# Two coupled transformer blocks in fp32: the turned rows of the first half moved by 32 bytes in SBUF

## The reference

```python
for l in range(2):                                  # first half; z likewise
    x = x + 0.5 * mx[2] * swiglu(modulate(rms_norm(x), mx[0], mx[1]), ffn1_w1[l], ffn1_w3[l], ffn1_w2[l])
    hx = modulate(rms_norm(x), mx[3], mx[4]) @ w_in[l]        # 1024 x 2336
    x = x + mx[5] * (token_mixing(hx, hz, ...) @ w_out[l])    # 1024 x 1024
    x = x + 0.5 * mx[8] * swiglu(modulate(rms_norm(x), mx[6], mx[7]), ffn2_w1[l], ffn2_w3[l], ffn2_w2[l])

def swiglu(h, w1, w3, w2):                          # w1, w3: 1024 x 2816; w2: 2816 x 1024
    return (jax.nn.silu(h @ w1) * (h @ w3)) @ w2
```

## Time and profile before

| | |
|---|---|
| median of 3 runs | 3195.55 us (3190.09 to 3196.07) |
| profiled execution | 3176.97 us |
| its span in the trace | 3175.2 us |
| TensorE matmul busy | 3051.7 us (96%) |
| TensorE weight load busy | 2772.3 us (87%) |
| VectorE, ScalarE, GpSimd busy | 1802.7, 1483.3 and 151.2 us |
| mean granted TensorE clock | 0.988 |
| DMA, share of 16 engines | 52% |

### The profile page before, as it was taken

One profiled execution on the slowest core, in us unless ns is written; L12 is line 12 of the kernel. 1 busy time (PEld: TensorE's weight loads), 2 busy tenths in 40 slices (PEclk: granted clock), 3 DMA queues, 4 the chain that ended last, 5 costly groups with the idle time before them and its releaser, 6 DMA issues.

```text
span 3175.2 us, 54273 instructions
## 1 busy us (share of the span) xinstructions
PE 3051.7 (96%) x23160; PEld 2772.3 (87%) x23160; DVE 1802.7 (57%) x2837; ACT 1483.3 (47%) x2222; POOL 151.2 (5%) x147
## 2 busy tenths in 40 slices
PE   7999999999999999999999999999999999999998
PEld 5899788898779997899898879999899999989997
DVE  4555554655456545545645455465766656586665
ACT  3344444453544443444444444455654445655443
POOL 0000000001000000000200000001010101111000
PEclk9999999999999999999999999999999999999999
DMA  7765444654445555765355345554355655434563
GB/s 272 283 212 171 149 151 169 216 196 145 143 153 186 174 190 192 271 222 163 133 172 166 114 159 201 189 176 134 115 161 183 198 187 164 126 111 162 173 199 133
DMA packets 409691, 556.67 MB, mean 175 GB/s; under 512 B 25276, under 2 KB 357996, under 8 KB 409068
## 3 DMA queue, kind: packets, MB, share of 16 engines
q1 hardware_dynamic: 409452, 553.20, 52.2%
HBM read 552.12 MB, written 1.05 MB: 174 GB/s over the span
## 4 chain that ended last, share of the span: by engine, by line
PE 83%; DVE 9%; ACT 3%; issue 3%; DMA 3%; SPq 0%; POOL 0%; DVEq 0%; ACTq 0%
PE psum L119 24%; PE psum L121 23%; PE psum L120 23%; DVE wl L276 1%; DMA wr<-in_ffn_w_dram 1%; PE psum L710 1%; DVE wl L2173 1%; PE psum L2338 1%; PE psum L2422 1%; PE psum L2444 1%; PE psum L1528 1%; PE psum L1183 1%; PE psum L127 1%; PE psum L1899 1%; PE psum L1515 1%
## 5 line engine op out<-in xcount | busy, mean ns | idle before, releaser
L276 DVE TENSOR_TENSOR wl<-wr,wh 128x1024 fp32r<-128x1024 f32 (+1 forms) x558 | 658.4, 1215 | 216.3 <-ACT wh L265 215.3
L265 ACT ACTIVATE wh<-wr 128x1024 fp32r<-128x1024 f32 (+1 forms) x558 | 555.0, 1039 | 249.4 <-DMA wr<-in_ffn_w_dram 219.7
L119 PE MATMUL psum<-xt_hi,wh 128*128 128x256 f32 (+1 forms) x2000 | 567.5, 284 | 4.7 <-DVE wl L276 3.7
L120 PE MATMUL psum<-xt_lo,wh 128*128 128x256 f32 (+1 forms) x2000 | 558.9, 279 | 0.0
L121 PE MATMUL psum<-xt_hi,wl 128*128 128x256 f32 (+1 forms) x2000 | 558.5, 279 | 0.0
L2173 DVE TENSOR_TENSOR wl<-wr,wh 128x1024 fp32r<-128x1024 f32 (+3 forms) x336 | 391.7, 1201 | 123.9 <-ACT wh L2165 122.6
L119 PEld LDWEIGHTS psum<-xt_hi,wh 128*128 128x128 f32 (+1 forms) x2000 | 377.7, 189 | 17.8 <-issue 10.9
L120 PEld LDWEIGHTS psum<-xt_lo,wh 128*128 128x128 f32 (+1 forms) x2000 | 377.4, 189 | 2.3
L121 PEld LDWEIGHTS psum<-xt_hi,wl 128*128 128x128 f32 (+1 forms) x2000 | 378.3, 189 | 0.1
L119 PE MATMUL psum<-wh,xt_hi 128*128 128x256 f32 (+1 forms) x1280 | 369.4, 289 | 2.8 <-ACT vv L3323 1.9
L2165 ACT ACTIVATE wh<-wr 128x1024 fp32r<-128x1024 f32 (+3 forms) x336 | 322.6, 997 | 102.4 <-DMA wr<-in_mlp_w_dram 75.2
(11 more groups left out here) (490 smaller groups left out, 5457.2 us busy)
## 6 DMA issues: line engine op xcount, KB each, us to landing
wr<-in_ffn_w_dram SPq DMA_DIRECT2D x231, 1024.0 KB, 5.2
wr<-in_w_in_dram SPq DMA_DIRECT2D x88, 1024.0 KB, 5.1
wr<-in_w_mod_dram SPq DMA_DIRECT2D x72, 1024.0 KB, 4.9
wr<-in_mlp_w_dram SPq DMA_DIRECT2D x64, 1024.0 KB, 5.3
wr<-in_w_out_dram SPq DMA_DIRECT2D x20, 1024.0 KB, 5.3
wr<-in_mem_w_kv_dram SPq DMA_DIRECT2D x8, 1024.0 KB, 5.2
wr<-in_w_branch_dram SPq DMA_DIRECT2D x16, 512.0 KB, 3.4
wr<-in_w_branch_dram SPq DMA_DIRECT2D x8, 1024.0 KB, 5.2
```

The lines of the kernel that those rows point to most:

```text
L119: pe.matmul(out, a[0], b[0], start=first, stop=False)
L120: pe.matmul(out, a[0], b[1], start=False, stop=False)
L265: act.activation(self.high[s][:, r], self.raw[s][:, r], ACT.Copy).then_inc(self.highs.sem, 1)
L276: dve.tensor_tensor(self.low[s][:, r], self.raw[s][:, r], self.high[s][:, r].bitcast(F32), ALU.subtract).then_inc(self.lows.sem, 1)
```

## The change

Three groups of tiles in the first half move by 32 bytes: the moved copies of `xt` and `zt` from 192 to 224 bytes below 80 KB and 64 KB, the scratch tiles that lie over them by as much, and the held copies from 64 to 32 bytes below 80 KB, and from 320 to 288 below 64 KB. Held less moved address becomes 128 less 32, so 96, in the up products, and 224 less 128, so 96, in the projections. The ring, the down products, `mem_t` and the second half keep their addresses. No instruction, wait or transfer is added or removed.

```diff
@@ -23,7 +23,7 @@
 SIDE_BANKS = 6
 MOD_COLS = 32
 RING_SHIFT, ROW_SHIFT = 3 / 8, 1 / 16
-MOVED_SHIFT, SIDE_SHIFT = 3 / 16, 3 / 16
+MOVED_SHIFT, HELD_SHIFT, SIDE_SHIFT = 7 / 32, 1 / 32, 7 / 32
 
 
 D_FF = 2816
@@ -3648,7 +3648,7 @@
     x = c["x"]
     pair = lambda name, kb: [at(name + "_hi", [P, KT, TOK], F32R, kb), at(name + "_lo", [P, KT, TOK], F32R, kb + 8)]
     moved = [pair("xt", 80 - MOVED_SHIFT), pair("zt", 64 - MOVED_SHIFT)]
-    held = [pair("xt", 80 - ROW_SHIFT), pair("zt", 64 - ROW_SHIFT - 1 / 4)]
+    held = [pair("xt", 80 - HELD_SHIFT), pair("zt", 64 - HELD_SHIFT - 1 / 4)]
     h = [at("hx", [P, 2, D_IN], F32, 130.5), at("hz", [P, 2, D_IN], F32, 112)]
     mix = at("mix", [P, 2, D], F32, 149)
     rows1, rows2, rtmp = at("gate_rows1", [P, D], F32, 157), at("gate_rows2", [P, D], F32, 161), at("gated_rows", [P, 512], F32, 165)
```

## The result

| | before | after |
|---|---|---|
| median of 7 runs | 3193.44 us | 3205.69 us |
| lowest and highest | 3174.26, 3196.07 us | 3197.61, 3212.65 us |
| ratio, 95% interval | | 1.0065 (1.0040 to 1.0089) |
| profiled execution | 3176.97 us | 3212.65 us |
| span in its trace | 3175.2 us | 3210.8 us |

The change makes the kernel slower by 0.65%: 21 us of 3193, with an interval of 13 to 28 us. I had forecast 14 us less. The ratio is the one on record; the two medians alone are 12 us apart (1.0038). Four runs of the kernel before were added to the three that stood ahead of the prediction; they moved its median by 2 us.

The account below looks back on a forecast made before the run. TensorE's rate of float32r products was taken to bound the kernel. All quick steps gave -14 us, other parts nothing; off the 3195.55 us median that made 3182 us, range 3168 to 3223.

Parts of the forecast that it names:

- What bounds the kernel: Whole kernel: TensorE, with matmuls in flight for 96% of the span; the rate of float32r products on lines 119 to 121.
- The two paces as states of a stretch: 256-column products: a stretch keeps the pace it gets into at its start, quick 113.3 ns or slow 117.8 ns a step.
- the step to 96 goes on in that direction: First-half up products and projections: moving away from 192 favours the quick pace, so all quick at 96, 14 us less.
- the sum: First-half up products and projections all quick at 113.3 ns, other parts costed at nothing: -14 us.
- the slower case: Lines 119 to 121, first-half up pieces: 96 behaves like 128, long stretches slow; 20 us more, 3215 us; chance 0.36.
- The chance of faster: Whole kernel: 0.44, from all quick or most of it at 0.35 and much faster at 0.09.
- wrong altogether: Sign: steps unchanged and time moving to side matmuls, writes of turned rows or low clock; or a third pace appears.
- The bound from above: First-half up products and projections: at most 118.3 ns a step, the mean at difference 128; over 9,184 steps 31 us more.
- The gain bound at 111.5 ns: First-half up products and projections: no faster than the second half's 160-column products; all at 111.5 gives 31 us less.
- Costed at nothing: Writes of the turned rows at other addresses, and side work on the moved scratch tiles (+-4 us for the range).
- Theory C: From the experiments, first half: the scratch tiles that moved along, or the work beside the stretches, make the difference.
- The rival that rested on the rule: No change: paces depend on what precedes a stretch, or 96 has the same mix as 64; 3195 us; chance 0.20.

## Why the prediction was wrong

*What bounds the kernel.* Right. The lines 119 to 121 set the time, the change acted on nothing but their rate, and the rate was to be read from start to start.

*The two paces as states of a stretch.* Right, and that made the effect measurable: a time of 3190 us scatters by 20 us from run to run, a mean over 7,092 steps does not.

*"For it: going from 192 to 64 turned up stretches from all slow to 38 of 45 quick, and the step to 96 goes on in that direction."* This is the step that failed. It made a slope out of two points of something that has none. The comparison itself was sound: 192 in the first half has 2 of 46 long up stretches quick. But 96 has none of 45, and its up steps have a mean of 118.41 ns where the sum had them at 113.3; 32, 48, 80, 128 and 0 have no quick long stretch either. The rows did not give a direction; they gave one difference with mostly quick stretches and two where the long ones were slow, and the honest reading was that a third, unseen, was more likely to be like the majority. I had put the same thought as "what lies nearest on the other side is slow" in the slower case, with 0.36, and taken the forecast from the other. The other half of the step, that the quick state is the one in which undisturbed stretches end, holds at 64 and not at 96. The chance of faster, 0.44, was too high on these rows. The sign of the slower case came (medians of 281 ns for `xt_lo,wh` and `zt_lo,wh`), and so did a third pace, 118.7 ns, and a fourth, 117.3, which the list of signs had put under wrong altogether. Why 96 has these paces and 64 others stays open.

*The sizes.* The bound from above was good. Up steps went to 118.41 ns, within 0.1 ns of the 118.3 of `ot_mla`, and all steps together to 31 us, the bound of 31 that I had worked out. That 96 falls so close to the 23 steps of another difference is luck: 128 itself came out at 119.0. The slower case with "half of the way to 128" took 20 us. In the runs 21 us came out (13 to 28), and in the traces 31 by steps and 36 by span. The two profiled executions lie to different sides of their medians, 16.5 us under and 7.0 us over; that is the gap between the 36 us of the traces and the 12 us between the medians. Why the runs of the kernel before spread from 3170 to 3201 us was not tried.

*The range*, 3168 to 3223, held the time, 3205.69 us, but it says little when it reaches to both signs.

*The gain bound at 111.5 ns* was never approached: no stretch of 256 columns went under 113.3.

*Costed at nothing.* Right: writes of the turned rows 686 and 687 ns for 687, side work without a trace of its own. Theory C gets no microsecond that the steps leave over.

*The rule of the Trainium skill* (SBUF — State Buffer, "Who interferes with whom"), that TensorE reads through two independent ports and waits on nobody, does not describe this kernel: with nothing changed but addresses, the long up stretches go from 113.4 ns for most of them (difference 64) to 119.9 for all (difference 0). That the two reads get in each other's way would fit, but no run shows where in TensorE or SBUF the time goes. The rival that rested on the rule got 0.20 and deserved less, as the earlier trace rows already said. One half of it holds: within one difference, what comes before a stretch can pick its pace, as `mem_t` shows.

## What to carry to other kernels

Where a stream of 128 x 128 by 256 float32r matmuls bounds a kernel, place the operands so that held less moved address is 64 modulo 256, the best of the eight differences tried here, and check it by steps from start to start rather than by time: 0.65% is hard to see in the time and plain in 7,000 steps. Two good-looking points do not make a slope; an effect that depends on addresses has to be scanned, and in steps finer than the one that first helped. A pace found in a trace may be one of several that the same addresses allow, so look at many stretches, and at what stands ahead of each. A tile used in two roles needs two copies if both roles are to have the right distance, which was worth 7 us by the steps where the second half had one.

## What the runs showed of the hardware that I had not expected

- The distance between the two operands sets the paces. At 64 most long up stretches run at 113.4 ns (38 of 45). At 0, 32, 48, 80, 96 and 128 none of 90 steps or more does; they run 3.9 to 6.6 ns slower, 3.4 to 5.8%, and one at 48 by 9.8 ns. At 192 both paces of 64 exist (113.3 and 117.8 ns), and 44 of 46 are slow.
- The state is remembered. At 64 the held copy of `xt` ran 359 steps at 113.3 ns, and in the same trace, from the same addresses, 431 steps at 117.8:

```profile
1462.14 0.28 PE L120 MATMUL psum<-wl,xt_hi 128*128 128x256 f32 x1
...
1512.90 0.28 PE L119 MATMUL psum<-xt_hi,wh 128*32 128x256 f32 x1
```

- It is carried from one piece to the next: the 47 steps of `mem_t` took the pace of the projection ahead of them in all 14 traces, once 117.9 ns and 13 times 113.3 to 113.4. Moving the down products by 64 bytes changed their own steps by under 1 ns and left 29 long up stretches quick for 38.
- With 512 moved columns the differences 64 and 128 are within 1 ns of each other (233.1 and 232.3 ns).
- A common shift does not matter, as far as it was tried: 32 bytes on everything left the means of the first half where they were, within 0.05 ns.
